# The start of a decoder layer: norm gain spread on chip, identity made on chip, loads issued in another order

## The chip, the cores and the metric

The kernel runs on 8 cores of one Trainium2 chip. Each core computes one of the eight sequences of the batch, and all eight run the same program. The metric is the device time in microseconds (us) of the slowest core. The time before is 937.29 us, the median of 3 runs (936.63 to 937.66).

## What is computed

One decoder layer over x of 2048 tokens by 1024, per sequence, cut to what matters here:

```python
h = rms_norm(x, norm_mix)                  # x * rsqrt(mean(x^2) + eps) * norm_mix
q, k, v, u, g_a, g_p = split(h @ w_in)     # q, k, v, u: 512 columns each
q = partial_rope(rms_norm(q_heads, q_norm)); k = partial_rope(rms_norm(k_heads, k_norm))
o_attn = block_sparse_attention(q, k, v)   # 8 heads of 64, blocks of 256, top 3 blocks
o_pool = multiscale_pool(u)
x = x + (sigmoid(g_a)*(o_attn@w_up_attn) + sigmoid(g_p)*(o_pool@w_up_pool)) @ w_out
x = x + relu(rms_norm(x, norm_mlp) @ w_ff1)^2 @ w_ff2
```

The change touches only the first stage: the norm of x, its transposition, and the projections to q, k, v and u.

## The kernel before, in words

**Helpers.** A class `Trk` keeps a semaphore for each engine and rings of semaphores for the DMAs of SyncE (`"sp"`) and of GpSimd (`"pool"`). Every operation goes through `t.op`, `t.group` (several matmuls that count as one) or `t.dma`; waits come from the buffers that an operation reads and writes. Each engine works through its own instructions in order. `t.wait_written(e, buf)` makes engine `e` wait until `buf` is written; everything behind it on that engine waits too.

**The work of the first stage.** x comes as 16 tiles of 128 tokens (512 KB of float32 each) into four slots (`p0_load`, SyncE's queue). For each tile ScalarE squares and sums it and takes the root (`p0_sq`, L388 and L391), VectorE takes the reciprocal (L397) and multiplies the tile by it and by the gain `gmix_bc` (`p0_mul`, L399). The bf16 result is transposed, for the first nine tiles by eight TensorE transposes (`p0_tr`, L406) that need the identity `ident_b` and a copy out of PSUM (`p0_ev`, L377 or L372), for the others by a DMA transpose. Then each of the four column groups K, V, Q and U has one job per tile: eight matmuls of 512 columns (`proj_mm`, L433), the first four with the first half of the weights, the other four with the second half. So there are 64 jobs. K and Q jobs are followed by a norm per head, a rotation and a transpose (L439 to L487), K and V and U by evictions.

**The weights** come by casting DMAs on GpSimd's queue, float32 in memory and bf16 on chip, two halves for each of K, V, Q and U (`load_w`; 512 KB written by each half).

**The order.** `first_loads` issues by hand what comes first. On SyncE: x tile 0, the gain `gmix_bc` (the 1024 gains copied to 128 rows by the host, 512 KB), then a wait for the first half of K's weights, then x tiles 1 and 2, three small tables (`c_small`, `c_gv`, `c_rope`) and x tile 3. On GpSimd: the identity (from memory), K's weights, five memsets (`pool_setup`, L353 and L355), a wait for x tile 1, V's weights.

All else is ordered by a planner that runs while the program is built. It gives each task a cost, an engine and an earliest time (`W_AT` for jobs by column group, `X_AT` for the first x tiles, `after` for others), simulates the five engines, and emits the tasks in the order of their simulated starts. Its numbers set only the order of the instructions; on the chip they wait for data. In its order, V's job of a tile lies 3 tiles behind K's, Q's 7 and U's 12. From tile 4 on a load of x waits for the multiplication that frees its slot. Q's weights are issued when the load into slot 0 that precedes them in program order (tile 4) has landed (`load_w_after`), U's with slot 1 (tile 5). When the projections near their end, the attention's steps begin (L907, L945).

Of the kernel before, what the change touches and what calls it, by code (L numbers as in the profile page):

```python
# [33 lines left out]
class Trk:  # L34
    def __init__(self, nc, es, n_ring=12):
# [9 lines left out]
        for q in ("sp", "pool"):  # L45
# [106 lines left out]
def build_nc():  # L152
    nc = bass.Bass("TRN2", target_bir_lowering=False)

    def din(name, shape):
# [21 lines left out]
    with es:  # L177
# [133 lines left out]
        b_wgTf, b_wgT, b_gmix_bc = Buf("wgTf"), Buf("wgT"), Buf("gmix_bc")  # L311
# [83 lines left out]
        def p0_mul(tt, s2):  # L395
# [6 lines left out]
                reads=[b_xslot[sl], b_rstd1[tt], b_gmix_bc], writes=[b_hb0[s2]])  # L402
# [221 lines left out]

        def first_loads():
            t.op("dve", lambda e: e.memset(eps_c, EPS), writes=[b_eps])
            t.op("dve", lambda e: e.memset(ones_b, 1.0), writes=[b_ones])
            p0_load(0)
            t.dma("pool", ident_b, c_ident_d, writes=[b_ident])
            t.dma("sp", gmix_bc, gmix_vec_d, writes=[b_gmix_bc])  # L630
            load_w(CG_K)
            pool_setup()
            t.wait_written("sp", b_wqkvu[CG_K][0])
# [6 lines left out]
            t.wait_written("pool", b_xslot[1])  # L640
# [8 lines left out]
        W_AT = {CG_K: 15.0, CG_V: 30.0, CG_Q: 43.0, CG_U: 54.0}  # L649
        X_AT = [4.7, 16.3, 18.6, 23.0]  # L650
# [822 lines left out]
```

How the kernel before makes its waits and increments, by code:

```python
    def _wait(self, e, need):  # L95
        eng = self.E[e]
        seen = self.seen[e]
        for k, v in need.items():
            if e == "pe" and k == "pe":
                continue
            if seen.get(k, 0) < v:
                eng.wait_ge(self.sems[k], v)
                seen[k] = v
# [9 lines left out]
    def op(self, e, fn, reads=(), writes=()):  # L113
        self._wait(e, self._need(reads, writes, e))
        ins = fn(self.E[e])
        self.cnt[e] += 1
        ins.then_inc(self.sems[e], 1)
        self._mark(e, self.cnt[e], reads, writes)
# [1 line left out]
    def group(self, e, fns, reads=(), writes=()):  # L120
        self._wait(e, self._need(reads, writes, e))
        ins = None
        for fn in fns:
            ins = fn(self.E[e])
        self.cnt[e] += 1
        ins.then_inc(self.sems[e], 1)
        self._mark(e, self.cnt[e], reads, writes)
# [1 line left out]
    def dma(self, q, out, in_, reads=(), writes=(), transpose=False):  # L129
        need = self._need(reads, writes)
        ring = self.rings[q]
        slot = ring["slots"][ring["i"] % len(ring["slots"])]
        ring["i"] += 1
        if slot[1] > 0:
            self._add(need, slot[0], slot[1])
        self._wait(q, need)
        if transpose:
            ins = self.E[q].dma_start_transpose(out=out, in_=in_)
        else:
            ins = self.E[q].dma_start(out=out, in_=in_)
        slot[1] += 16
        ins.then_inc(self.sems[slot[0]], 16)
        self._mark(slot[0], slot[1], reads, writes)
```

## Time and profile before

| what | value |
|---|---|
| median of 3 runs | 937.29 us |
| the profiled execution, its own time | 936.56 us |
| its span on the slowest core (core 4) | 935.5 us, so 1.06 us lie around it |
| spans of the eight cores | 930.1 to 935.5 us |
| TensorE (matmul) busy | 899.7 us, 96% of the span |
| VectorE, ScalarE busy | 462.3 us (49%), 364.8 us (39%) |
| GpSimd busy | 111.8 us (12%) |
| data moved by DMA | 78.13 MB, mean 84 GB/s |

In the rows, PE is TensorE, PEld its weight loads, DVE VectorE, ACT ScalarE, POOL GpSimd, SP SyncE; a q behind a name is that engine's queue of instructions. A time is in us from the start of the span unless marked ns. L12 is a line of the kernel. A matmul that waits behind others in the pipeline counts as busy, so a busy PE need not be one at its peak. A row of the chain of waits names what the end of a stretch hung on, step by step.

### The profile page before, as it was taken

Reading aid. Unit: us, or ns where it says so; the run is one execution under the profiler, and the core shown is the slowest. Engines: PE = TensorE matmul, PEld = TensorE weight load, DVE = VectorE, ACT = ScalarE, POOL = GpSimd, SP = SyncE. Lnnn points to the kernel's source line nnn. Section 1 sums busy time; section 2 is a strip of 40 time slices with the busy share of each in tenths; the row PEclk is TensorE's granted clock in tenths of the full one; section 3 lists DMA queues with packets and bytes.
Section 4 is the critical chain, followed back from the end, with each engine's and each line's share of the span. In section 5 each row is a group of like instructions: output and inputs, shape, how many; then the busy total and the mean of one; then the engine's idle time right before and its main releaser. Section 6 shows DMA issues by size and latency. Waiting matters only on the chain.

```text
span 935.5 us, 17328 instructions; the slowest of 8 cores (930.1 to 935.5 us)
## 1 busy us (share of the span) xinstructions
PE 899.7 (96%) x5724; PEld 461.8 (49%) x5724; DVE 462.3 (49%) x870; ACT 364.8 (39%) x722; POOL 111.8 (12%) x197
## 2 busy tenths in 40 slices
PE   2899998999999999999999999999999999999998
PEld 1444454667777654444444444444444444444444
DVE  2788877647332233345774444444443444444443
ACT  3777455788999952221006223131101222111120
POOL 4212212221000000100201111001110111000000
PEclk9999999999999999999999999999999999999999
DMA  7963353244533363993996433023330333202113
GB/s 186 226 160 80 64 136 46 53 63 75 70 69 66 61 102 98 203 197 83 159 142 99 56 48 55 12 32 48 56 46 1 46 47 56 34 1 82 54 68 157
DMA packets 66342, 78.13 MB, mean 84 GB/s; under 512 B 35984, under 2 KB 54672, under 8 KB 66000
## 3 DMA queue, kind: packets, MB, share of 16 engines
q0 software_dynamic: 25056, 40.28, 28.9%
q1 hardware_dynamic: 41200, 36.75, 16.5%
q8 instruction: 48, 0.79, 0.3%
q14 instruction: 38, 0.31, 0.1%
HBM read 98.41 MB, written 8.39 MB: 114 GB/s over the span
## 4 chain that ended last, share of the span: by engine, by line
PE 88%; DMA 6%; DVE 2%; issue 1%; ACT 1%; SPq 0%; POOL 0%; DVEq 0%; ACTq 0%; POOLq 0%
PE bank L1370 24%; PE bank L1341 24%; PE bank L1013 11%; PE bank L433 8%; PE bank L1241 6%; PE bank L907 6%; PE bank L945 3%; DMA raw<-w_qkvu 3%; PE bank L1027 3%; PE bank L1032 3%; DMA raw<-x 2%; DMA raw<-w_slice 1%; PE bank L487 1%; PE bank L520 0%; DVE raw L377 0%
## 5 line engine op out<-in xcount | busy, mean ns | idle before, releaser
L1370 PE MATMUL bank<-raw 128*128 128x512 bf16 (+1 forms) x1032 | 223.2, 377 | 0.0
L1341 PE MATMUL bank<-raw 128*128 128x512 bf16 x1024 | 223.1, 379 | 0.0
L1348 ACT ACTIVATE raw<-bank 128x512 f32<-128x512 f32 x128 | 76.4, 597 | 375.6 <-PE bank L1341 317.0
L1370 PEld LDWEIGHTS bank<-raw 128*128 128x128 bf16 x1032 | 101.1, 98 | 120.2
L1341 PEld LDWEIGHTS bank<-raw 128*128 128x128 bf16 x1024 | 100.1, 98 | 120.9
L1350 DVE SCALAR_TENSOR_TENSOR raw<-bank,raw 128x512 bf16<-128x512 f32 x128 | 88.5, 692 | 140.0 <-ACT raw L1348 140.0
L914 ACT ACTIVATE raw<-bank 128x512 bf16<-128x512 f32 (+1 forms) x288 | 145.0, 580 | 24.6 <-PE bank L945 20.6
L1378 DVE SCALAR_TENSOR_TENSOR raw<-bank,raw 128x512 f32<-128x512 f32 x129 | 96.3, 746 | 113.5 <-PE bank L1370 112.8
L433 PE MATMUL bank<-raw 128*128 128x512 bf16 x512 | 121.2, 386 | 10.9 <-ACT raw L372 3.8
L1013 PE MATMUL bank<-raw 128*128 128x512 bf16 x512 | 123.0, 380 | 2.1 <-DMA raw<-w_slice 1.9
L907 PE MATMUL bank<-raw 128*128 128x256 bf16 x576 | 98.7, 268 | 0.8 <-ACT raw L914 0.3
L140 POOL DMA_DIRECT2D raw<-w_ff x64 | 44.9, 702 | 347.2 <-PE bank L1341 184.9
L945 PEld LDWEIGHTS bank<-raw 128*128 128x128 bf16 x1088 | 69.9, 98 | 26.0 <-issue 1.0
L945 PE MATMUL bank<-raw 128*128 128x65 bf16 x1088 | 80.0, 194 | 0.8 <-DVE raw L954 0.7
L433 PEld LDWEIGHTS bank<-raw 128*128 128x128 bf16 x512 | 47.7, 98 | 66.0 <-issue 17.4
L1038 DVE SCALAR_TENSOR_TENSOR raw<-raw,bank 128x512 f32<-128x512 f32 x64 | 43.7, 685 | 71.5 <-PE bank L1032 53.8
L1013 PEld LDWEIGHTS bank<-raw 128*128 128x128 bf16 x512 | 49.4, 98 | 51.0 <-issue 3.2
L1018 ACT ACTIVATE raw<-bank 128x512 f32<-128x512 f32 x64 | 38.2, 597 | 75.2 <-PE bank L1013 73.9
L1241 PE MATMUL bank<-raw 128*128 128x512 bf16 x256 | 55.4, 379 | 0.0
L1241 PEld LDWEIGHTS bank<-raw 128*128 128x128 bf16 x256 | 25.0, 98 | 30.2
L907 PEld LDWEIGHTS bank<-raw 128*128 128x128 bf16 x576 | 37.1, 98 | 2.4 <-issue 1.2
L1027 PE MATMUL bank<-raw 128*128 128x512 bf16 x128 | 32.9, 379 | 0.0
(90 smaller groups left out, 578.2 us busy)
## 6 DMA issues: line engine op xcount, KB each, us to landing
raw<-x SPq DMA_DIRECT2D x32, 512.0 KB, 7.0
raw<-w_ff POOLq DMA_DIRECT2D x64, 256.0 KB, 4.0
raw<-w_slice POOLq DMA_DIRECT2D x22, 640.0 KB, 7.9
out<-raw SPq DMA_DIRECT2D x15, 512.0 KB, 2.7
raw<-w_qkvu POOLq DMA_DIRECT2D x8, 512.0 KB, 13.2
raw<-raw SPq DMA_DIRECT2D x2, 1024.0 KB, 4.5
raw<-w_out POOLq DMA_DIRECT2D x4, 512.0 KB, 13.1
raw<-c_ind POOLq DMA_DIRECT2D x4, 256.0 KB, 5.2
```

What stands on the lines that cost most here:

```text
L433: t.group("pe", [lambda e, c=c: e.matmul(bank_f(bk), lhsT=hT[:, c, tt * 128:(tt + 1) * 128], rhs=wqkvu[cg][:, c, :], start=(c == 0), stop= ...
L907: fns.append(lambda e, kt=kt, j=j, qa=qa: e.matmul(bank_f(sb_)[:, j * 256:j * 256 + 256 - qa], lhsT=ksel[:, pr, kt * 128:(kt + 1) * 128], ...
L914: t.op("act", lambda e: e.activation(out=pt[:, 0:nc_], in_=bank_f(sb_)[:, 0:nc_], func=AF.Exp, scale=0.125), reads=hb[sb_], writes=[b_PT[s ...
L945: fns.append(lambda e, dst=dst, c0_=c0_, kt=kt, ql=ql, last=last: e.matmul(dst, lhsT=pt[:, c0_:c0_ + 128], rhs=v_aug[:, kt, h, :], start=( ...
L1013: t.group("pe", [lambda e, c=c: e.matmul(bank_f(bk), lhsT=w[:, c, :], rhs=hT[:, c, T0:T0 + 512], start=(c == 0), stop=(c == 7)) for c in c ...
L1027: t.group("pe", [lambda e, c=c: e.matmul(bank_f(bk), lhsT=w[:, c, :], rhs=o_attnT[:, c, T0:T0 + 512], start=(c == 0), stop=(c == 3)) for c ...
L1241: t.group("pe", [lambda e, c=c, bk=bk, hf=hf: e.matmul(bank_f(bk), lhsT=mT[tt // 4][:, c, (tt % 4) * 128:(tt % 4 + 1) * 128], rhs=wout[:, ...
L1341: t.group("pe", [lambda e, c=c, j=j, bk=bk: e.matmul(bank_f(bk), lhsT=ffw1[s][:, c, j * 128:(j + 1) * 128], rhs=hT[:, c, tg * 512:(tg + 1) ...
L1348: t.op("act", lambda e, bk=bk, si_=si_: e.activation(out=sqz[si_], in_=bank_f(bk), func=AF.Square), reads=hb[bk], writes=[b_sqz[si_]])
L1350: t.op("dve", lambda e, bk=bk, si_=si_, j=j: e.scalar_tensor_tensor(out=a1T[ab][:, j, :], in0=bank_f(bk), scalar=0.0, in1=sqz[si_], op0=AL ...
L1370: t.group("pe", [lambda e, j=j, bk=bk, i=i, c0_=c0_, c1_=c1_, n_=n_: e.matmul(bank_f(bk)[:, 0:n_], lhsT=a1T[ab][:, j, i * 128:(i + 1) * 12 ...
L1378: t.op("dve", lambda e, bk=bk, dst=dst, tt=tt, n_=n_: e.scalar_tensor_tensor(out=dst, in0=bank_f(bk)[:, 0:n_], scalar=r2sq[:, tt:tt + 1], ...
```

## The change

1. The host passes the 1024 gains as [8, 128] (4 KB) in place of [128, 1024]. They are loaded into `g8` by a DMA on ScalarE's queue. VectorE splits them into three bf16 parts (three copies, two subtractions, each 8 x 128), TensorE spreads them over 128 rows with 24 matmuls (three for each 128 columns; the left operand is a column of the identity, read 128 times), and VectorE copies the two PSUM banks to `gmix_bc`.
2. The identity isn't loaded: GpSimd makes it with a memset and two affine selects, ahead of K's weights.
3. ScalarE runs a one-column Square of `eps_c` first of all, so that its table load doesn't wait for x.
4. On SyncE x tiles 1 and 2, the tables and x tile 3 no longer wait for K's weights. On GpSimd V's weights wait for the second half of K's and no longer for x tile 1. U's weights wait for slot 2 (tile 6) in place of slot 1.
5. The K jobs of tiles 0 and 1 are two tasks each, one for each half of the weights.
6. The planner's earliest times are lower: for K's jobs 12.5 in place of 15 (their first halves 9), for V, Q and U 6 lower each, for x tiles 1 to 3 8.2, 11.5 and 15.5 in place of 16.3, 18.6 and 23.0. VectorE counts as free from 7.

```diff
-        for q in ("sp", "pool"):
+        for q in ("sp", "pool", "act"):
...
-    gmix_vec_d = din("gmix_bc", [128, D])
+    gmix_vec_d = din("gmix", [8, 128])
-    c_ident_d = din("c_ident", [128, 128])
...
+        def spread_gain():
+            src, bsrc = g8, b_g8
+            for i in range(3):
+                t.op("dve", lambda e, i=i, src=src: e.tensor_copy(out=g8p[i], in_=src),
+                     reads=[bsrc], writes=[b_g8p[i]])
+                if i < 2:
+                    t.op("dve", lambda e, i=i, src=src: e.tensor_tensor(
+                        out=g8r[i], in0=src, in1=g8p[i], op=ALU.subtract),
+                        reads=[bsrc, b_g8p[i]], writes=[b_g8r[i]])
+                    src, bsrc = g8r[i], b_g8r[i]
+            for hf in range(2):
+                bk = gbank[hf]
+                fns = []
+                for c in range(4 * hf, 4 * hf + 4):
+                    for i in range(3):
+                        fns.append(lambda e, c=c, i=i, bk=bk: e.matmul(
+                            bank_f(bk)[:, (c % 4) * 128:(c % 4) * 128 + 128],
+                            lhsT=ident_b[0:8, c:c + 1].to_broadcast([8, 128]), rhs=g8p[i],
+                            start=(i == 0), stop=(i == 2)))
+                t.group("pe", fns, reads=[b_ident] + b_g8p, writes=hb[bk])
+                evict(("dve", "dve")[hf], gmix_bc[:, hf * 512:hf * 512 + 512], bank_f(bk), hb[bk], [b_gmix_bc[hf]])
+            for i in range(3):
+                b_qtok[i].fence = {"pe": t.cnt["pe"], "dve": t.cnt["dve"]}
         def first_loads():
             t.op("dve", lambda e: e.memset(eps_c, EPS), writes=[b_eps])
             t.op("dve", lambda e: e.memset(ones_b, 1.0), writes=[b_ones])
+            t.op("act", lambda e: e.activation(out=junk[:, 0:1], in_=eps_c, func=AF.Square),
+                 reads=[b_eps], writes=[b_junk])
+            t.dma("act", g8, gmix_vec_d, writes=[b_g8])
             p0_load(0)
-            t.dma("pool", ident_b, c_ident_d, writes=[b_ident])
-            t.dma("sp", gmix_bc, gmix_vec_d, writes=[b_gmix_bc])
+            t.op("pool", lambda e: e.memset(ident_b, 1.0), writes=[b_ident])
+            t.op("pool", lambda e: e.affine_select(
+                out=ident_b, in_=ident_b, pattern=[[1, 128]], compare_op=ALU.is_ge, fill=0.0, base=0,
+                channel_multiplier=-1), reads=[b_ident], writes=[b_ident])
+            t.op("pool", lambda e: e.affine_select(
+                out=ident_b, in_=ident_b, pattern=[[-1, 128]], compare_op=ALU.is_ge, fill=0.0, base=0,
+                channel_multiplier=1), reads=[b_ident], writes=[b_ident])
             load_w(CG_K)
+            spread_gain()
             pool_setup()
-            t.wait_written("sp", b_wqkvu[CG_K][0])
             p0_load(1)
             p0_load(2)
...
             p0_load(3)
-            t.wait_written("pool", b_xslot[1])
+            t.wait_written("pool", b_wqkvu[CG_K][1])
             load_w(CG_V)
...
-        W_AT = {CG_K: 15.0, CG_V: 30.0, CG_Q: 43.0, CG_U: 54.0}
-        X_AT = [4.7, 16.3, 18.6, 23.0]
+        K0_AT = 9.0
+        W_AT = {CG_K: 12.5, CG_V: 24.0, CG_Q: 37.0, CG_U: 48.0}
+        X_AT = [4.7, 8.2, 11.5, 15.5]
...
-            gains[is_k] = add("gains", pr_, [("dve", 0.85, lambda is_k=is_k: setup_gains(is_k))], after=20.5)
+            gains[is_k] = add("gains", pr_, [("dve", 0.85, lambda is_k=is_k: setup_gains(is_k))], after=14.5)
...
+            if cg == CG_K and tt < 2:
+                ph = Task("half", ji - 0.5, [], deps=[hev[tt]], get=["pj"], after=K0_AT)
+                ph.opts = [("pe", 0.87, lambda ji=ji, k_=ph: proj_mm(ji, k_.slots["pj"], (0,)))]
+                tasks.append(ph)
+                pj.deps, pj.get, pj.slots = [ph], [], ph.slots
+                pj.opts = [("pe", 0.87, lambda ji=ji, k_=pj: proj_mm(ji, k_.slots["pj"], (1,)))]
...
-        add("wq", 4.0, [("pool", 2.0, lambda: load_w_after(CG_Q, 0))], deps=[muls[1]], after=26.0)
-        add("wu", 8.0, [("pool", 2.0, lambda: load_w_after(CG_U, 1))], deps=[muls[2]], after=34.0)
+        add("wq", 4.0, [("pool", 2.0, lambda: load_w_after(CG_Q, 0))], deps=[muls[1]], after=25.0)
+        add("wu", 8.0, [("pool", 2.0, lambda: load_w_after(CG_U, 2))], deps=[muls[3]], after=34.0)
...
-        eng_free = {"pe": 0.0, "act": 0.0, "dve": 0.0, "pool": 20.0, "sp": 22.0}
+        eng_free = {"pe": 0.0, "act": 0.0, "dve": 7.0, "pool": 14.0, "sp": 15.0}
```

## Rows read from the trace of the kernel before

**Rows 1.** Projection matmuls (L433) by 5 us: stretch, length, busy, count, clock, DMA share, GB/s

```profile
10.00:15.00 5.00, 1.86 (x4) 1.00 0.96 193
...
35.00:40.00 5.00, 2.45 (x11) 1.00 1.03 222
...
100.00:105.00 5.00, 4.94 (x23) 1.00 0.55 107
```

**Rows 2.** The chain of waits, 0 to 40 us: start, length, what

```profile
2.24 9.53 DMA raw<-w_qkvu
11.85 4.63 DMA raw<-x
...
17.53 16.87 DMA raw<-w_qkvu
...
35.86 0.47 PE bank L406 x8
36.33 1.73 PE bank L433 x8
```

**Rows 3.** The timeline, 0 to 34 us: start, length, what, idle before it

```profile
1.07 0.40 SPq L140 DMA_DIRECT2D raw<-x  x1
...
1.53 0.41 SPq L140 DMA_DIRECT2D raw<-gmix_bc  x1
...
3.54 7.92 POOL L355 MEMSET raw<- 128x2048 f32 x4
5.11 1.28 ACT L388 ACT_TABLE_LOAD   x1 [5.11 <-DMA raw<-x]
...
8.44 1.28 DVE L399 SCALAR_TENSOR_TENSOR raw<-raw 128x1024 bf16<-128x1024 f32 x1 [0.17 <-DVE raw L397]
...
9.98 1.01 PE L406 MATMUL bank<-raw 128*128 128x128 bf16 x8 [9.98 <-DVE raw L399]
...
12.04 1.86 PE L433 MATMUL bank<-raw 128*128 128x512 bf16 x4 [1.05 <-DVE raw L377]
...
15.44 1.87 PE L433 MATMUL bank<-raw 128*128 128x512 bf16 x4 [1.53 <-DMA raw<-w_qkvu]
...
17.01 1.06 POOL L140 DMA_DIRECT2D raw<-w_qkvu  x2 [5.54 <-DMA raw<-x]
...
23.57 1.06 ACT L388 ACTIVATE raw<-raw 128x1024 bf16<-128x1024 f32 x1 [1.35 <-DMA raw<-x]
...
25.15 0.22 DVE L474 TENSOR_TENSOR raw<-raw 128x64 f32<-128x64 f32 x1
25.47 0.23 DVE L477 TENSOR_TENSOR raw<-raw 128x64 f32<-128x64 f32 x1
...
27.36 1.06 POOL L140 DMA_DIRECT2D raw<-w_qkvu  x2 [9.29 <-DMA raw<-x]
...
27.86 1.89 PE L433 MATMUL bank<-raw 128*128 128x512 bf16 x8 [0.75 <-ACT raw L372]
```

**Rows 4.** DMA queues' packets, MB, share, in the microsecond from 7, 17, 22 and 23

```profile
q0 software_dynamic: 47, 0.14, 118.2%
...
q1 hardware_dynamic: 120, 0.05, 17.2%
...
q1 hardware_dynamic: 101, 0.35, 92.2%
...
q0 software_dynamic: 18, 0.07, 47.6%
```

**Rows 5.** The weights' DMA queue from 25 to 30 us

```profile
q0 software_dynamic: 156, 0.57, 67.4%
```

**Rows 6.** GpSimd: an instruction by form, and those of L477, duration min/median/max

```profile
L359 POOL TENSOR_SCALAR_AFFINE_SELECT raw<-raw 128x128 bf16<-128x128 bf16 x1 | 0.3, 293 | 0.1
...
L477 POOL TENSOR_TENSOR raw<-raw x11: 317/319/1284, 32.5 to 124.4; 128x64 f32<-128x64 f32 x11
```

**Rows 7.** Busy time from 60 to 80 us: PE, PEld, DVE, ACT, POOL

```profile
60.00:80.00 20.00, 19.26 (x118) 9.42 (x117) 17.63 (x46) 14.16 (x30) 5.92 (x13) 1.00 0.50 107
```

**Rows 8.** TensorE's timeline where the attention begins

```profile
151.04 0.33 PE L907 MATMUL bank<-raw 128*128 128x256 bf16 x2
```

More of the change, by code:

```diff
@@ L266, in build_nc @@
         gmix_bc = view(E0 + 2 * KB, [128, D], F32)
+        g8 = view(E0 + 14 * KB, [8, 128], F32)
+        g8r = [view(E0 + 14 * KB + 512, [8, 128], F32), view(E0 + 15 * KB, [8, 128], F32)]
+        g8p = [view(E0 + 15 * KB + 512 + i * 256, [8, 128], BF16) for i in range(2)]
+        g8p.append(view(E0 + 16 * KB, [8, 128], BF16))
         hb0 = [view(o_, [128, D], BF16) for o_ in (E0 + 6 * KB, E0 + 8 * KB, G0 + 3584)]
@@ L310, in build_nc @@
         b_ones, b_band, b_qz, b_tri, b_eps = Buf("ones"), Buf("band"), Buf("qz"), Buf("tri"), Buf("eps")
-        b_wgTf, b_wgT, b_gmix_bc = Buf("wgTf"), Buf("wgT"), Buf("gmix_bc")
+        b_wgTf, b_wgT = Buf("wgTf"), Buf("wgT")
+        b_gmix_bc = [Buf("gmix_bc%d" % i) for i in range(2)]
         b_xslot = [Buf("xslot%d" % i) for i in range(NXS)]
@@ L401, in p0_mul @@
                 op0=ALU.mult, op1=ALU.mult),
-                reads=[b_xslot[sl], b_rstd1[tt], b_gmix_bc], writes=[b_hb0[s2]])
+                reads=[b_xslot[sl], b_rstd1[tt]] + b_gmix_bc, writes=[b_hb0[s2]])
         def p0_tr(tt, s2, bk):
@@ L429, in build_nc, with proj_mm @@
         NJ = len(jobs)
-        def proj_mm(ji, bk):
+        def proj_mm(ji, bk, hfs=(0, 1)):
             cg, tt = jobs[ji]
-            for hf in range(2):
+            for hf in hfs:
                 t.group("pe", [lambda e, c=c: e.matmul(
@@ L623, in build_nc @@
                  "st": [0, 1, 2, 3], "x16": [0, 1], "qtok": [0, 1, 2], "u": list(range(NU)), "mb": [3]}
+        b_g8, b_g8r, b_g8p = Buf("g8"), [Buf("g8r%d" % i) for i in range(2)], [Buf("g8p%d" % i) for i in range(3)]
+        def spread_gain():
[21 more added lines that the diff above has]
+                b_qtok[i].fence = {"pe": t.cnt["pe"], "dve": t.cnt["dve"]}
         def first_loads():
@@ L1409, in _host_consts @@
 def _host_consts():
-    ident = np.eye(128, dtype=np.float32)
     half = 8
@@ L1429, in _host_consts @@
         band[:, g * 3 + 2, :] = main0
-    return ident, rope, band
+    return rope, band
 _CACHE = {}
@@ L1437 @@
     x = f(x)
-    ident, rope, band = _host_consts()
+    rope, band = _host_consts()
     gq, gk = f(q_norm)[0], f(k_norm)[0]
@@ L1458 @@
         "c_small": small, "c_gv": gv, "gmlp_bc": np.ascontiguousarray(np.broadcast_to(f(norm_mlp)[0], (128, D))),
-        "gmix_bc": np.ascontiguousarray(np.broadcast_to(f(norm_mix)[0], (128, D))),
-        "c_ident": ident, "c_rope": rope, "c_band": band,
+        "gmix": f(norm_mix)[0].reshape(8, 128),
+        "c_rope": rope, "c_band": band,
         "c_ind": ind4,
```

## The prediction

> **What bounds the kernel now.** The page says TensorE is busy for 96% of the span, so time can only come from stretches in which it isn't fed. I looked for them first with the projection matmuls counted by 5 us [rows 1]. Eight of them, a job, take 1.73 us when nothing waits [rows 2], so 23 fit into 5 us; the count is 4 from 10 to 15 us, 11 from 35 to 40 and 23 from 100 to 105. By 40.4 us six jobs (10.4 us), six tile transposes (0.47 each [rows 2], 2.8) and about 0.9 us of small ones are done: 14.1 us of work, so some 26.3 us are lost. From there to 151 us, where the attention's steps begin [rows 8], lie 110.6 us; 55 jobs take 95.2 of them and the transposes and band matmuls beside them about 12.5, so about 3 more are lost, 29.3 in all. A gain in the start therefore isn't eaten up by TensorE later: it works without gaps and only begins earlier. That is the main reason why I expect the whole span to follow.
>
> What the lost 26 us hang on is in the chain of waits [rows 2]: K's weights to 11.8 us, then x tile 1 (issued only after them), then V's weights, issued behind that tile and landed at 34.4 us. Three DMAs make up 31 of the first 34.4 us; VectorE and ScalarE are not in that part of the chain. The timeline [rows 3] gives the steps between: the table load begins only when x tile 0 is there (5.11), first multiplication at 8.44, first projection matmul at 12.04, second half of K at 15.44.
>
> **How fast the two DMA queues are.** The queue of x alone moves about 100 packets of 4 KB per us (a tile is 128), the weights' queue alone 47 in the stretch shown, some of them small, and with both at work the weights get 156 in 5 us, 31 per us [rows 4, 5]. A column group's weights are 256 packets, so 8.3 us of data. K's ran from about 5.3 to 14.1 with x mostly absent, 8.8 us, which is no faster. So letting x in beside K costs K little. That is where I chose: the bound on the good side is K's second half at 15.0 us, on the bad side a K that waits behind x (a rival below).
>
> Two more facts of the same rows. At 17 us the x queue is at 17%: the small tables hold x tile 3 up while nothing else runs. And V, issued at 17.01 [rows 3], has its first 18 packets only in the stretch from 23 us [rows 4], 6 us later, when the x tiles queued ahead of it are nearly through. K's issue at 2.24 had its first at about 5.3, when x tile 0 and the gain (issued at 1.07 and 1.53) were through. I read both as: a weight load starts about 3 us after its issue, or when the x packets queued before it have drained, if that is later.
>
> The Trainium skill (DMA: Bandwidth & Descriptors, Queues, rings and completion order) says that each DMA engine goes round between its queues packet by packet. By that alone V would have started 3 us after its issue. From 25 us on the trace agrees (31 of each per us); for the start it doesn't. With the round alone, V's data would begin 1 us sooner than I take below, and the sum would be 1 us lower.
>
> **The parts.**
>
> *Gain spread.* Removed: 512 KB from x's queue (128 packets, 1.3 us at 100 per us). Added on the path of tile 0: ScalarE's table load from about 1.25 to 2.55 and a short Square, DMA issue to about 3.1. No such small transfer on a queue of its own is in the trace. x tile 0 was issued at 1.07 and there at 5.11, 4.0 us with 1.8 us of data, so 2.2 without them; the old gain took 5.5 us behind it. So it lands between 5.3 and 8.6; I take 5.3, as it has no data to speak of. Five dependent VectorE operations of 128 columns: between the 0.06 us of a one-column memset and the 0.32 us from one start to the next of L474 and L477 [rows 3]; I take 0.32, the nearest, 1.6 us, so 6.9. 24 matmuls of 128 columns at the slow pace of the first transposes (8 in 1.01, so 0.11 apart [rows 3]): 2.6 us, and the last copy out 0.69: about 10.4. Then reciprocal and the multiplication, which began at 8.44 before: 10.8 now. The transposes and copy that follow put the first projection matmul at 14.4 in place of 12.04. This part makes the start 2.4 us later. It costs nothing in the sum, because the second tile's multiplication could not begin before 18.5 then (tile 1 landed at 16.5 [rows 2]) and now tile 1 is there at about 7, where the gain landed before. Without that cover it would cost 2.4.
>
> *Table load.* 1.28 us [rows 3] leave the path of tile 0, but that path now ends in the gain. Worth 0.
>
> *Identity.* One DMA issue (0.68) goes; a memset (0.2) and two selects (0.29 each [rows 6]) plus their hand-overs come, ahead of K's issue: between 0.3 sooner and 0.5 us later. I take 0.1 later. GpSimd's memsets, 7.92 us, move with it and still end before V's issue.
>
> *x tiles at once.* SyncE's issues of tiles 1 and 2, the tables and tile 3 now run from about 1.5 us. Tile 1 takes the place of the gain (7), tile 2 comes at about 11, the tables by 16, tile 3 at 17.5 in place of 23.5, tile 4 (once the first multiplication has freed its slot, 12) at about 20 in place of 27.3 [rows 3].
>
> *V behind K.* K's data start at 5.4, take 8.3 us and land 1.4 us after their last packet (as 15.44 lay behind 14.1), so its second half lands at 15.2, the issue of V follows at 15.7 in place of 17.01. x tiles 3 and 4 are ahead of it and drain by 19.5; data to 27.8, landed at about 29.2 in place of 34.4. Q and U follow on the same queue without a gap, as they did. **This is the term that counts: 5.2 us.**
>
> *TensorE between 14.4 and 29.2.* K jobs of tiles 0 to 4: 8.65 us, five tile transposes 2.35, four head transposes 1.2, and the slow pace: the first 16 matmuls were 0.43 apart in place of 0.22 (4 in 1.86 at 12.04, 8 in 1.89 at 27.86 [rows 3]; 1.2 GHz and then 2.4 GHz, the column of the granted clock being at 1.00 in both), so up to 4.3 us. Together 16.5 us for 14.8 us: TensorE is just fed. Its lost time would then be 14.4 + 4.3 and 4.5 us of later gaps (the 3 of before and 1.5 for a late x tile), 23.2, against 29.3 before: 6.1 us. The two countings give 5.2 and 6.1; I take 5.2, the one that has its end in a DMA. Halves of K jobs: they let four matmuls run before K's second half; in my times the second half is there (15.2) before the first has run (16.2), so nothing.
>
> **Sum.** The profiled execution took 936.56 us (span 935.5): 936.56 - 5.2 = 931.4. The median of the runs is 0.73 higher than that execution, so I forecast 932.1.
>
> **Rivals.**
> - *V's wait only moves* (0.16). If V starts 6.3 us after its issue as before, whatever is ahead, it gains only the 1.3 us of its issue; TensorE is then ahead by a job or so of K (1.73): 3.0 us, 934.3. For it: only one such start is in the trace. Against: the K load started in 3 us.
> - *Port between VectorE and GpSimd* (0.10). Shown: L477 on GpSimd took 1284 ns once in place of 319, under a 1.28 us multiplication on VectorE [rows 6]. Under the four memsets (1.98 us apart) the three copies of the gain split could each wait for one to end: the chain ends near 9.5 in place of 6.9 and the first projection is at 17. Of the 2.6 us some 2 would be lost: 934.1. Against: the multiplication at 8.44 ran its normal 1.28 under a memset. The Trainium skill (SBUF — State Buffer, Who interferes with whom) has it as an exclusive lock for one-source copies between SBUF tiles; no row before has such a copy.
> - *VectorE is the true bound of the stage* (0.09): it is busy for 17.63 of the 20 us from 60 to 80 [rows 7]. Then an earlier TensorE only waits more: under 1 us gained, 936.6. Against: VectorE starts earlier as well.
> - *Slower: K behind x* (0.06). If K's packets wait until all x packets issued before them are through (tiles 0 to 3 and the rope table, 640 packets at 100, and the tables' stall of 2.7 us), they start at 11.8 in place of 5.3, K lands at 22, V is issued at 22.5 and lands near 38: 3.6 us later than now, 940.9. It decides from the point where K's second half lands later than about 17.5. The start rule above leans this way; against it, SyncE needs about 0.45 us for each issue and is not far ahead of GpSimd's issue.
> - The rest (0.59) is the forecast, with 0.06 of it beyond 7.8 us, should TensorE be fed from 12 us.
>
> **Range.** Low end 929.5 (7.8 us gained: the 6.1 of the second counting, 1 for the start of V's data and some luck in the new order); high end 936.0 (the two middle rivals with 1.5 us against them). About 0.06 lie below and 0.13 above. Within 0.2% (1.9 us, about what a measurement of this kernel can tell from no change) counts the VectorE rival and a rest of the first: 0.11; slower 0.06; faster 0.83.
>
> **What the profile after would show.** First multiplication near 10.8 and first projection near 14.4; tile 1's square at about 7; V landed at 29 in place of 34.4; over 30 projection matmuls before 30 us in place of 25 or so; no x queue at 17% alone; attention's first step 5 us earlier than 151. I am wrong if V lands after 32 us, if K's second half lands after 17.5, or if gaps between 40 and 150 us grow beyond 3 us.

## The result, and the profile after

The kernel after takes 945.83 us (median of 4 runs, 943.94 to 974.86); the kernel before, timed beside it, 937.34. The ratio is 1.0085, with an interval of 1.0065 to 1.0105. (At 974.86 the cores of one die ran at a lower clock; ratios leave such executions out, medians don't.) The change makes the kernel about 8 us **slower**; the forecast was 932.1.

| what | before | after |
|---|---|---|
| the profiled execution, its own time | 936.56 us | 945.19 us |
| span of the core shown | 935.5 (core 4) | 943.5 (core 6) |
| first projection matmul | 12.04 | 17.20 |
| K's weights landed, halves 1 and 2 | 11.8 and 15.3 | 14.2 and 20.1 |
| V's weights landed, halves 1 and 2 | 29.6 and 34.4 | 28.2 and 33.3 |
| first halves of Q's and U's weights landed | 38.9, 48.3 | 38.2, 47.6 |
| x tiles 1, 2, 3, 4, 5 landed | 16.5, 18.7, 23.5, 26.8, 31.5 | 7.1, 8.8, 21.6, 22.9, 24.1 |
| x tiles 8, 9, 12 landed | 45.7, 50.4, 59.0 | 43.2, 48.7, 58.2 |
| granted clock, mean of the core | 0.998 | 0.994 |

**The start.** The timeline of the kernel after, 0 to 34 us (start, length, what, the idle time before it and what ended that). It answers to [rows 3]. The lines have moved: L433 is now L437 (projections), L406 L410 (tile transposes), L388 L392 (square of x), L399 L403 (multiplication), L439 L443 (square of a K or Q job), L461 L465 (the last read of a job's PSUM bank), L907 L953.

```profile
1.27 1.28 ACT L659 ACT_TABLE_LOAD   x1 [1.27 <-DVE raw L658]
...
2.35 1.23 POOL L140 DMA_DIRECT2D raw<-w_qkvu  x2 [0.23 <-issue]
...
3.81 7.91 POOL L359 MEMSET raw<- 128x2048 f32 x4
...
5.06 0.97 DVE L635 CAST raw<-raw 8x128 bf16<-8x128 f32 x1 [3.83 <-DMA raw<-gmix]
...
6.52 1.43 DVE L635 CAST raw<-raw 8x128 bf16<-8x128 f32 x1
...
8.44 1.44 DVE L635 CAST raw<-raw 8x128 bf16<-8x128 f32 x1
...
10.02 2.71 PE L647 MATMUL bank<-raw 8*128 8x128 bf16 x24 [10.02 <-DVE raw L635]
...
13.70 1.28 DVE L403 SCALAR_TENSOR_TENSOR raw<-raw 128x1024 bf16<-128x1024 f32 x1
...
17.20 1.87 PE L437 MATMUL bank<-raw 128*128 128x512 bf16 x4 [1.05 <-DVE raw L401]
...
20.24 3.25 PE L437 MATMUL bank<-raw 128*128 128x512 bf16 x12 [0.32 <-DMA raw<-w_qkvu]
...
20.63 1.05 POOL L140 DMA_DIRECT2D raw<-w_qkvu  x2 [8.91 <-DMA raw<-w_qkvu]
...
33.45 0.81 PE L437 MATMUL bank<-raw 128*128 128x512 bf16 x3 [0.39 <-DMA raw<-w_qkvu]
```

The table load is off the path, as forecast. The three casts of 8 x 128 took 0.97, 1.43 and 1.44 us, each beside one of GpSimd's memsets: they end at 6.03, 7.95 and 9.87, each within 0.1 us of the end of a memset (5.95, 7.88, 9.80). So the first multiplication came at 13.70 (forecast 10.8). K's second half was there at 20.1 (forecast 15.2), so V's issue came at 20.63, 3.6 us *later* than before, and V landed at 33.3 (forecast 29.2). The core shown is a late one: over the eight cores K's second half landed between 16.8 and 20.3 (before: 15.1 to 16.0).

The DMA queues of the kernel after in the microsecond from 9 (packets, MB, share), in answer to [rows 4]:

```profile
q0 software_dynamic: 33, 0.14, 90.5%
q1 hardware_dynamic: 32, 0.00, 5.0%
```

K's queue (q0) had its first 5 packets in the microsecond from 7, when x tiles 0 to 2 were all but through, 5 us after the issue at 2.35; its steady stream begins at 7.9. From then on it got one packet for each of x's queue (q1), here the small tables, 32 packets that carry next to nothing. That alone didn't make K slow. In the three microseconds from 11 four cores (1, 3, 4, 7) moved 34 to 44 of K's 4 KB packets per us beside as many small ones, no fewer than K got alone before (27 to 44 per us from 8 to 12 us); on the other four, the shown one with them, K fell to 12 to 24. Why it did stays open.

**The stage.** Projection matmuls (L437) of the kernel after by 5 us, columns as in [rows 1]: length, busy, count, the same two for the weight loads, granted clock, DMA share, GB/s.

```profile
10.00:15.00 5.00, 0.00 (x0) 0.00 (x0) 1.00 0.94 97
...
35.00:40.00 5.00, 4.81 (x22) 1.84 (x20) 1.00 0.99 216
...
50.00:55.00 5.00, 3.45 (x17) 1.40 (x16) 1.00 1.01 233
55.00:60.00 5.00, 1.53 (x8) 0.49 (x5) 0.88 0.54 163
60.00:65.00 5.00, 3.57 (x8) 1.02 (x8) 0.50 0.42 129
65.00:70.00 5.00, 4.48 (x20) 1.91 (x21) 0.93 0.00 0
...
100.00:105.00 5.00, 4.26 (x20) 1.80 (x20) 1.00 0.27 52
```

From 35 to 40 us there are 22 matmuls where there were 11: the start is indeed ahead by then. But from 55 to 65 us there are 16, half of them at a granted clock of 0.50, TensorE's 1.2 GHz level. The kernel before has 45 there, at 1.00 (columns as in [rows 1]):

```profile
55.00:60.00 5.00, 4.55 (x22) 1.00 0.45 157
60.00:65.00 5.00, 4.84 (x23) 1.00 0.17 47
```

To see where the kernels part I count the start of the n-th projection matmul, the median of the cores whose trace has all 512:

```
n          1     33     65     97    129    193    257    449    512
before   12.3   33.2   44.1   51.8   60.1   76.1   93.3  141.1  158.4
after    17.2   32.0   40.8   49.4   64.7   80.6   99.7  146.5  166.6
later    +4.9   -1.2   -3.3   -2.4   +4.6   +4.5   +6.4   +5.4   +8.2
```

The 8.2 us at the end of the stage are about the loss of the whole kernel. **They are made of** a head start of 2.4 us at the 97th matmul, 7.0 lost up to the 129th, 1.9 from the 193rd to the 257th, 2.8 at the end (449th to 512th), and 1.1 won back between.

The first of these is the largest. TensorE's timeline and then ScalarE's, of the same stretch:

```profile
54.65 1.89 PE L437 MATMUL bank<-raw 128*128 128x512 bf16 x8
60.94 3.57 PE L437 MATMUL bank<-raw 128*128 128x512 bf16 x8 [4.41 <-DVE raw L465]
```

```profile
53.60 1.06 ACT L392 ACTIVATE raw<-raw 128x1024 bf16<-128x1024 f32 x1 [2.49 <-DMA raw<-x]
...
55.05 0.58 ACT L443 ACTIVATE raw<-bank 128x512 f32<-128x512 f32 x1
57.11 1.06 ACT L392 ACTIVATE raw<-raw 128x1024 bf16<-128x1024 f32 x1 [1.49 <-DMA raw<-x]
...
58.55 0.58 ACT L443 ACTIVATE raw<-bank 128x512 f32<-128x512 f32 x1
59.03 0.29 ACT L452 ACTIVATE raw<-raw 128x8 f32<-128x8 f32 x1
...
59.79 0.59 ACT L443 ACTIVATE raw<-bank 128x512 f32<-128x512 f32 x1
```

ScalarE waits for an x tile that has not landed (2.49 and 1.49 us) while the squares (L443) and roots (L452) of finished K and Q jobs stand behind it in its order. The job squared at 55.05 was summed by VectorE from 55.72 and got its root only at 59.03, behind the square of the x tile at 57.11. Without the root there is no scaling (L465), so the job's PSUM bank isn't freed, and TensorE stops for 4.41 us; its next eight matmuls take 3.57 us in place of 1.73. The chain of waits of the kernel after says it in one line (start, length, what), and has the second loss as well:

```profile
46.04 10.99 DMA raw<-x
57.11 1.16 ACT raw L392 x2
...
76.72 6.82 DMA raw<-x
```

**Why the order is wrong.** The order is the planner's, and the change lowered its numbers (part 6 of the change). Its own simulated times beside the chip's, for the square of an x tile, in us:

```
x tile                   3      9     10     11     12
before, planned       23.0   45.2   50.2   53.0   55.9
before, on the chip   23.6   50.5   54.8   57.8   60.1
after, planned        15.5   38.4   41.0   43.1   46.9
after, on the chip    22.4   48.8   53.6   57.1   60.3
```

Before, the plan was 4 to 5 us ahead of x; after, 10 to 14. On the chip tile 12 is squared at the same time in both.

### The profile page after: what moved, and what is told of

The parts are those of the page before. It is cut to its first block, busy times and chain, and to the rows that moved or that the text cites. A ratio compares the mean times of both kernels' runs of the same rounds, so it can differ in the third digit from the quotient of the medians.

```text
span 943.0 us, 17387 instructions; the slowest of 8 cores (939.2 to 943.5 us)
## 1 busy us (share of the span) xinstructions
PE 903.5 (96%) x5748; PEld 463.8 (49%) x5748; DVE 469.3 (50%) x884; ACT 366.7 (39%) x728; POOL 107.0 (11%) x187
## 4 chain that ended last, share of the span: by engine, by line
PE 88%; DMA 6%; DVE 3%; issue 2%; ACT 1%; POOL 0%; SPq 0%; DVEq 0%; ACTq 0%; POOLq 0%
PE bank L1416 23%; PE bank L1387 23%; PE bank L1059 11%; PE bank L437 8%; PE bank L953 6%; PE bank L1287 6%; PE bank L991 3%; DMA raw<-w_qkvu 3%; PE bank L1073 3%; PE bank L1078 3%; DMA raw<-x 2%; DMA raw<-w_slice 1%; PE bank L491 1%; PE bank L524 0%; DVE raw L381 0%
## 5 line engine op out<-in xcount | busy, mean ns | idle before, releaser
L437 PE MATMUL bank<-raw 128*128 128x512 bf16 x512 | 122.1, 389 | 14.4 <-DVE raw L465 7.9
L953 PE MATMUL bank<-raw 128*128 128x256 bf16 x576 | 98.6, 267 | 0.6 <-ACT raw L960 0.2
L437 PEld LDWEIGHTS bank<-raw 128*128 128x128 bf16 x512 | 47.9, 99 | 70.0 <-issue 22.2
L953 PEld LDWEIGHTS bank<-raw 128*128 128x128 bf16 x576 | 36.9, 97 | 2.0 <-issue 0.9
```

Of the source, the lines that this page charges most:

```text
L437: t.group("pe", [lambda e, c=c: e.matmul(bank_f(bk), lhsT=hT[:, c, tt * 128:(tt + 1) * 128], rhs=wqkvu[cg][:, c, :], start=(c == 0), stop= ...
L953: fns.append(lambda e, kt=kt, j=j, qa=qa: e.matmul(bank_f(sb_)[:, j * 256:j * 256 + 256 - qa], lhsT=ksel[:, pr, kt * 128:(kt + 1) * 128], ...
```

## The experiments

Sixteen runs, each a ratio to the kernel before timed in the same session; medians of different sessions are not compared with each other. In the later sessions the kernel before took 1.4 to 2.3 us more than in that of its profile (937.3), so differences under about 2 us from the row `before` in the tables below prove little.

**The change with the planner's old numbers** (`a_plan_old`), and the kernel before with the new ones (`b_plan_new`).

```diff
-        K0_AT = 9.0                                  # the kernel after
-        W_AT = {CG_K: 12.5, CG_V: 24.0, CG_Q: 37.0, CG_U: 48.0}
-        X_AT = [4.7, 8.2, 11.5, 15.5]
+        K0_AT = 12.0                                 # a_plan_old
+        W_AT = {CG_K: 15.0, CG_V: 30.0, CG_Q: 43.0, CG_U: 54.0}
+        X_AT = [4.7, 16.3, 18.6, 23.0]
```

Beside these, each took the other's `after` times, `eng_free` and slot for U's weights.

> The changed loads, spread gain and split K jobs, with the planner's numbers of the kernel before (first halves of K at 12). Theory 1, the order: the changed kernel is ahead of the one before up to the 97th projection matmul (49.4 against 51.8 us) and behind by 4.6 us at the 129th, after ScalarE sat in front of the squares of x tiles that had not landed; the new order assumes x and weights 6 to 7 us earlier than they come. With the old numbers the gap of 4.4 us near 56 us goes and the time falls to 934 to 938. Theory 2, the loads themselves (K's weights landing at 20 in place of 15.4, V's only 1 us sooner): the time stays at 943 to 946.

> The kernel before with only the planner's numbers of the changed one (and U's weights behind x slot 2); loads, gain and identity as before. Theory 1 (the order): slower than before by 5 to 9 us, 942 to 946, with a gap of some us near 55 us in front of a projection matmul. Theory 2 (the loads): within 2 us of before, 936 to 939.

Measured: a 943.61 us, ratio 1.0037 (1.0021 to 1.0052); b 948.43 us, 1.0096 (1.0074 to 1.0118). The numbers alone, on the old loads, cost as much as the whole change. In b, TensorE's timeline and ScalarE's have the same stop:

```profile
64.22 3.57 PE L433 MATMUL bank<-raw 128*128 128x512 bf16 x8 [4.20 <-DVE raw L461]
```

```profile
60.40 1.06 ACT L388 ACTIVATE raw<-raw 128x1024 bf16<-128x1024 f32 x1 [2.81 <-DMA raw<-x]
...
61.84 0.58 ACT L439 ACTIVATE raw<-bank 128x512 f32<-128x512 f32 x1
```

The old numbers don't fit the new loads either. In a, ScalarE squares tile 1, which landed near 7, only behind the square of the first K job, and that waits for K's late weights:

```profile
22.39 0.60 ACT L443 ACTIVATE raw<-bank 128x512 f32<-128x512 f32 x1 [16.09 <-PE bank L437]
22.89 1.05 ACT L392 ACTIVATE raw<-raw 128x1024 bf16<-128x1024 f32 x1
```

**The kernel before with half of the new numbers**: x's (`h_x_only`) or the weights' (`h_w_only`).

```diff
-        X_AT = [4.7, 16.3, 18.6, 23.0]               # h_x_only; "sp" also free from 15
+        X_AT = [4.7, 8.2, 11.5, 15.5]
-        W_AT = {CG_K: 15.0, CG_V: 30.0, CG_Q: 43.0, CG_U: 54.0}    # h_w_only
+        W_AT = {CG_K: 12.5, CG_V: 24.0, CG_Q: 37.0, CG_U: 48.0}
```

> The kernel before with only the planner's arrival times of x of the changed one (tiles at 8.2, 11.5, 15.5, SyncE free from 15). With all of the new numbers the kernel before took 9.6 us more. If it is the x times, this is slower by 6 to 10 us; if it is the weights' times, it is within 2 us of before. The planner puts the x squares at up to 13 us ahead of the landing with these, so I expect most of the loss here.

> The kernel before with only the planner's times of the weights of the changed one (12.5, 24, 37, 48). If the weights' times make the loss, slower by 6 to 10 us; else within 3 us: TensorE waits in its own queue for a job whose weights come 6 us later, but what stands behind it waits for tiles anyway.

Measured: 957.43 us, ratio 1.0184 (1.0154 to 1.0214), and 950.6 us, 1.0111 (1.0091 to 1.013). Numbers that only put the same instructions in another order cost up to 1.8%. x's half costs more than I expected and more than both halves together (b). Each has the same wait of ScalarE for x, first h_x_only, then h_w_only; TensorE's stops behind them are 5.66 and 2.78 us:

```profile
64.68 1.06 ACT L388 ACTIVATE raw<-raw 128x1024 bf16<-128x1024 f32 x1 [6.58 <-DMA raw<-x]
```

```profile
58.80 1.06 ACT L388 ACTIVATE raw<-raw 128x1024 bf16<-128x1024 f32 x1 [4.24 <-DMA raw<-x]
```

**All of the planner's numbers set to what the chip did** (`e_plan_true`), and **one of them alone** (`m_after_x43`), or that one and the first x tiles (`n_after_x_true`).

```diff
-        W_AT = {CG_K: 12.5, CG_V: 24.0, CG_Q: 37.0, CG_U: 48.0}    # e_plan_true
-        X_AT = [4.7, 8.2, 11.5, 15.5]
+        W_AT = {CG_K: 20.2, CG_V: 31.0, CG_Q: 40.0, CG_U: 50.0}
+        X_AT = [4.9, 7.2, 8.9, 21.7]                 # n_after_x_true too
...
-                x_ld[tt] = add("xld", pk - 9, [("sp", 2.6, lambda tt=tt: p0_load(tt))],
+                x_ld[tt] = add("xld", pk - 9, [("sp", 4.3, lambda tt=tt: p0_load(tt))],   # all three
```

> The changed kernel; only the planner's numbers are other ones, taken from where the changed kernel's data really land (x tiles 4.9, 7.2, 8.9, 21.7; K 15.5 and 20.2, V 31, Q 40, U 50; a later x load 4.3 us in place of 2.6; VectorE free from 13.4). Theory 1 (the order assumes data 6 to 13 us too early, so ScalarE waits for x tiles in front of work that TensorE needs): the 129th projection matmul comes at 58 to 61 in place of 64.7 us, the ratio to before falls from 1.0085 to 0.998 to 1.002. Theory 2 (what the loads do in the first 20 us costs by itself): the ratio stays above 1.004.

> The kernel after, with one number of the planner changed: a load of x from tile 4 on costs 4.3 us on its queue in place of 2.6. In the planner's own times the square of x tile 9 then stands at 43.6 (38.4 before this edit), tile 12's at 58.8 (46.9); on the chip the kernel after had them at 48.8 and 60.3. Theory (ScalarE's order runs ahead of x and TensorE stops for 4.4 us): the stop near 56.5 us goes, the 97th and 129th projection matmul are 10 to 12 us apart in place of 15.3, and the time is 939 to 942, a ratio of 0.999 to 1.003. Rival (it is the numbers of the weights and of the first four x tiles, which stay too early): the stop stays, 945. Second rival (the loads themselves cost the time): 945 too, but with the 97th to 129th matmul as in the kernel before.

> The kernel after, with the load cost of 4.3 us and the first x tiles planned where they land (4.9, 7.2, 8.9, 21.7), the weights' numbers left too early (K 9 and 12.5, V 24, Q 37, U 48). Theory: x's order is what counts, so this is within 0.15% of the run with all numbers true (939). Rival (the weights' early numbers alone cost, as in the old kernel with them, where they cost 1.1%): 943 to 948.

Measured: e 938.99 us, ratio 0.9992 (0.9978 to 1.0005); m 940.34 us, 1.0010 (0.9994 to 1.0025); n 941.48 us, 1.0023 (1.0011 to 1.0036). One number, the 2.6 us that the planner takes for a load of x, carries the most: with 4.3 the ratio falls from 1.0085 to 1.0010. ScalarE's and TensorE's timelines of m have neither the wait for x nor the stop:

```profile
52.43 1.05 ACT L392 ACTIVATE raw<-raw 128x1024 bf16<-128x1024 f32 x1
...
53.86 0.58 ACT L443 ACTIVATE raw<-bank 128x512 f32<-128x512 f32 x1
...
56.65 1.05 ACT L392 ACTIVATE raw<-raw 128x1024 bf16<-128x1024 f32 x1
```

```profile
54.17 5.34 PE L437 MATMUL bank<-raw 128*128 128x512 bf16 x24
```

The matmuls of these runs, n-th start as above:

```
n            1     33     65     97    129    193    257    449    512
before     12.3   33.2   44.1   51.8   60.1   76.1   93.3  141.1  158.4
after      17.2   32.0   40.8   49.4   64.7   80.6   99.7  146.5  166.6
a          17.2   38.9   48.1   56.2   64.2   84.0  102.2  149.0  166.3
b          21.2   35.1   43.4   52.0   66.7   82.6  102.2  149.0  168.5
e          17.6   33.0   41.4   50.0   60.0   77.4   93.9  141.9  159.2
m          17.2   32.3   43.4   51.9   59.9   78.3   95.6  142.9  163.3
n          17.4   36.2   44.4   52.8   60.9   76.8   94.3  141.8  162.6
```

The last column isn't the kernel's loss to the microsecond: a ends the stage 7.9 us later and the kernel is 3.5 us slower by its ratio, m 4.9 and 0.9; 1.4 to 1.6 us of that may be the sessions'. n was expected within 0.15% of e and isn't. The table shows where: at the 449th matmul n is level with e; the last 64 take 20.8 us in n, 20.4 in m and 20.1 in the kernel after, 17.3 in e and before.

**The hand-over to the attention** (`j_hand`, `k_g_hand`). That end loss is a second stop, in TensorE's timeline of the kernel after:

```profile
157.98 0.71 PE L953 MATMUL bank<-raw 128*128 128x256 bf16 x6
160.69 3.08 PE L437 MATMUL bank<-raw 128*128 128x512 bf16 x8 [2.01 <-DVE raw L465]
```

Six score matmuls stand together and the next job then waits 2.01 us for its bank, at a lower clock behind; before, the scores came two at a time, from 151.04 on [rows 8]. My theory was that the attention is begun too early in the plan.

```diff
-        T_ATT = last_root.end + LAT
+        T_ATT = last_root.end + LAT + 2.0            # k_g_hand: the same on g_loads
```

> The changed kernel with the attention's first steps put 2 us later into the order. In it the 449th projection matmul is 5.4 us later than before and the 512th 8.2, with a gap of 2.2 us near 158 us. If where the attention's steps are mixed in costs these 2.8 us, they go and the ratio falls by 0.002 to 0.003 from 1.0085; if the earlier loss is all, the ratio stays.

> The same 2 us in g_loads, where the 449th matmul was 1.0 us earlier than before and the 512th 1.7 later. If the hand-over costs it 2.7 us: ratio 0.997 to 0.999 in place of 1.0004. If not: 1.000 to 1.002.

Measured: 949.07 us, ratio 1.0108 (1.0079 to 1.0137), and 941.55 us, 1.0025 (1.0009 to 1.0041), no better than the kernels they started from. The theory falls: the last 64 matmuls still take 20.2 us in j.

What the slow ends have in common is a PSUM bank. The last five U jobs may use banks 6 and 7 alone (`pj.only = gbank`). Worked out from each kernel's own planner, the last Q job, whose bank is held until its scaling (L465), stands in one of these two or outside them, and the time of the last 64 matmuls goes by that without an exception:

```
last Q job in bank 6 or 7    after 20.1, b 19.5, c 20.4, d 21.0, g 20.0, h_x 20.1, j 20.2, k 21.3, m 20.4, n 20.8
last Q job in bank 4 or 5    before 17.3, a 17.3, e 17.3, h_w 17.6, i 17.4, l 17.3, o 17.3, p 17.3
```

The job that starts at 160.69 is the first of the five in bank 7, and it starts when the last Q job's L465 (159.87, 0.68 us) is through. So some 3 us of the kernel after, and most of what parts n from e, go with the bank that the rotation had reached, and not with how true the numbers are. No run changed the bank alone.

**The loads.** With the order set aside, is anything in the loads worth having? First the gain's casts on ScalarE (`c_act_cast`), and the tables behind x tile 3 (`d_tables_late`), both on the kernel after.

```diff
-                t.op("dve", lambda e, i=i, src=src: e.tensor_copy(out=g8p[i], in_=src),
+                t.op("act", lambda e, i=i, src=src: e.activation(out=g8p[i], in_=src, func=AF.Copy),
```

```diff
             p0_load(2)
+            p0_load(3)
             t.dma("sp", small_c, c_small_d, writes=[b_small, b_gcq, b_gck])
...
-            p0_load(3)
```

> The changed kernel with the three bf16 copies of the gain split on ScalarE in place of VectorE. If VectorE's copies wait for GpSimd's memsets (they took 0.97, 1.43 and 1.44 us for 128 columns of 8 rows), the copies take about 0.3 us each, the first gain matmul comes at 7.5 in place of 10.0 and the first projection at about 14.7 in place of 17.2; the second half of K still lands near 20, so the time changes by less than 1.5 us. If the copies are slow for another reason, they stay above 0.9 us.

> The changed kernel with the three small tables behind x tile 3 on SyncE. In the changed kernel the 256 small packets of two tables ran one by one with K's packets from 8 to 18 us and x tile 3 stood behind them (landed at 21.6). Here x tile 3 lands by about 11, K's first packet comes 1 to 1.5 us later (9), K lands at 21, the tables at 20 to 22. If the loads of the first 20 us are what costs (theory 2), 2 to 3 us are gained by the earlier tile 3 or lost by the later K; by theory 1 (the order further on) the time stays within 1.5 us of 945.

Measured: c 944.8 us, ratio 1.0056 (1.0036 to 1.0075); d 945.93 us, 1.0068 (1.0043 to 1.0093). Two lines of c's timeline:

```profile
5.79 0.31 ACT L635 ACTIVATE raw<-raw 8x128 bf16<-8x128 f32 x1 [3.01 <-DMA raw<-gmix]
...
14.99 1.44 PE L437 MATMUL bank<-raw 128*128 128x512 bf16 x3 [1.05 <-DVE raw L401]
```

A cast takes 0.31 us on ScalarE in place of 0.97 to 1.44, and the first projection comes 2.2 us earlier; but from the 33rd matmul to the 97th c is within 0.1 us of the kernel after. In d, x tile 3 landed at 16.7 in place of 21.6 and V's issue came at 19.06; at the 97th matmul it is 0.9 us behind the kernel after. Neither interval lies apart from that of the kernel after.

Then **loads in an order that gives K its old place** (`g_loads`: tables on ScalarE's queue, x tile 1 with K, tiles 2 and 3 behind K's first half, casts on ScalarE, numbers to match), and **V issued right behind K** (`i_v_behind`: g without V's wait). On the mended order, the casts alone (`o_e_act`: e with them on ScalarE).

```diff
+            t.dma("act", small_c, c_small_d, writes=[b_small, b_gcq, b_gck])      # g_loads, i_v_behind
+            t.dma("act", gv_qk, c_gv_d.partition_broadcast(128), writes=[b_gv])
+            t.dma("act", rope_t, c_rope_d.rearrange("p (t n) -> p t n", t=NT), writes=[b_rope])
...
+            p0_load(1)
...
+            t.wait_written("sp", b_wqkvu[CG_K][0])
...
-            t.wait_written("pool", b_wqkvu[CG_K][1])                              # i_v_behind alone
```

> The changed kernel with other loads and true planner numbers for them: x tile 1 beside K, x tiles 2 and 3 after K's first half, the small tables on ScalarE's queue, the gain's copies on ScalarE. Expected: K lands at 12 and 15.5 as before, x tile 3 at 17.5, V issued at 16 and landed at 28, first projection near 14.5. Theory 1 plus 2: both costs gone, the last projection matmul 4 to 6 us earlier than before and the ratio 0.993 to 0.996. If the ratio is 1.0 or more, the stage's end isn't set by its first 30 us at all.

> The loads of g_loads, but V's weights are issued right behind K's and GpSimd's memsets (no wait), so the weights' queue has no hole (in the kernel before it had none of its packets from 14 to 23 us). Planner numbers for it (K 13 and 16.5, V 25, Q 34.5, U 43, x tiles 6, 8.3, 18, 22, then 4.2 us each). If the stage is set by when V, Q and U land: V lands at 21 to 26 in place of 30 to 35, the 65th projection matmul comes at 38 to 41 in place of 44.1, the last one 3 to 5 us earlier than before, the ratio 0.994 to 0.998. If it is set by the x tiles (31 packets per us beside weights) and the hand-over to the attention: ratio 0.999 to 1.003.

> The kernel after with all of the planner's numbers set to the landings (the run at 939.0) and the three gain copies on ScalarE, where they took 0.31 us each in place of 1.0 to 1.4. The first projection then begins near 15 in place of 17.6. If the start is worth what it gains: 937 (2 us less, since the second half of K lands at 20 whatever comes before, perhaps 1). If the stage is paced by x and its order (my theory now): within 0.1% of that run, 938 to 940.

Measured: g 940.43 us, ratio 1.0004 (0.9991 to 1.0016); i 941.25 us, 1.0019 (1.0004 to 1.0034); o 937.22 us, 0.9987 (0.9964 to 1.0009). g didn't give K its old place on every core: on core 4 K's halves landed at 13.2 and 16.6 and V's at 29.7 and 35.0, no earlier than before (29.6 and 34.4); the median of the eight is 18.1 for K's second half. It is 1.0 us ahead at the 449th matmul and loses that in the slow end. i has V's halves at 23.8 and 28.2 on core 4, about 6 us earlier, and then x tiles 2 to 5 only at 26.3 to 32.2, so TensorE has nothing to project; its timeline in i:

```profile
29.67 1.01 PE L410 MATMUL bank<-raw 128*128 128x128 bf16 x8 [7.77 <-DVE raw L459]
```

In o the first projection comes 3.0 us earlier than in e (14.6), the 512th 1.3 us (157.9); the intervals of the two overlap, and neither is apart from the kernel before. Why so little of a head start carries is one line in the chain of waits of e:

```profile
43.71 9.97 DMA raw<-x
```

From 44 to 54 us the chain hangs on x. o has the same line, 9.50 us from 41.20; g, m, n and l have none between 35 and 100 us, so it is not the rule for every order. e is 2.7 us ahead of the kernel before at the 65th matmul, 1.8 at the 97th, 0.1 at the 129th.

**The kernel before, its order alone made truer** (`l_before_x43`, and once more, `p_before_x43_again`).

```diff
-                x_ld[tt] = add("xld", pk - 9, [("sp", 2.6, lambda tt=tt: p0_load(tt))],
+                x_ld[tt] = add("xld", pk - 9, [("sp", 4.3, lambda tt=tt: p0_load(tt))],
```

> The kernel before with only the planner's cost of a later x load at 4.3 us in place of 2.6, what 31 packets per us beside the weights make of a tile of 128 packets (and near what the trace shows between landings from 27 to 55 us). If the order's misfit to the data is what costs, this is 0 to 2 us faster than before (its own x squares stood up to 5 us ahead of the landings); if the planner's numbers only shuffle the order by luck, it may be some us slower.

> The kernel before with only the planner's cost of an x load raised from 2.6 to 4.3 us, run once more on another chip: a ratio of 0.997 to 0.999 if the 0.22% gain of the first run is real, 1.000 if it was chance.

Measured: 937.22 us, ratio 0.9978 (0.9966 to 0.9991), and 936.67 us, 0.9974 (0.9961 to 0.9986). One number, with no part of the change, beats the kernel before by a quarter per cent, and no version of the change is apart below that (e 0.9992 and o 0.9987 overlap with it). The profiled executions don't show where: the 512th projection matmul starts at 158.8 and 158.9 (before 158.4, profiled in a faster session). That stays open.

## Why the prediction was wrong

**The step that failed** is the one I called my main reason: "A gain in the start therefore isn't eaten up by TensorE later: it works without gaps and only begins earlier." It was read from a trace in which it was true. It held because the planner's order fitted the old landings to within about 5 us, and the change moved that order too. What the runs showed in its place: TensorE was 2.4 us ahead at the 97th projection matmul, 4.6 us behind at the 129th and 8.2 behind at the 512th. I priced the planner's numbers nowhere in the sum. Their cost: 0.96% on the old loads (b), and with all of them true the 0.85% of the whole change goes to nothing (e); some 3 us of that go with the bank of the last Q job. The mechanism is a wait that no step of mine priced: that of all that is queued behind ScalarE's square of an x tile. The Trainium skill (PSUM — Partial Sum Buffer, Engine vs sequencer instructions) says that ScalarE's, VectorE's and GpSimd's queues are strict FIFO; the timeline agrees, L443 and L452 starting only when L392 is through, with their input ready.

**The head start isn't worth much even so.** I read the chain of waits only to 40 us. Had I read on, the kernel before has the same line (start, length, what):

```profile
50.24 7.52 DMA raw<-x
```

The DMA share of the kernel before is 1.02 to 1.04 in each 5 us from 20 to 55 us, and in the kernel after 0.99 to 1.05: the DMA engines are full, and x tile 12 lands at 58.2 in place of 59.0 though tile 1 is 9.4 us earlier. By these shares only bytes moved before 20 us, or not moved at all, would bring it forward. The gain's 512 KB and the identity's 32 are all that went; the stretch in which the x queue idled is now full of packets, but from 10 to 15 us they carry 97 GB/s in place of 193.

Point by point, by the prediction's own steps:

- *V behind K*, 5.2 us, "the term that counts": 1.1 us were measured (34.4 to 33.3). K's second half landed at 20.1, not 15.2. "Letting x in beside K costs K little" was wrong in the start, K beginning behind x tiles 0 to 2 (7.9 us, not 5.4). In the rate it was right on four cores; on the other four K fell to 12 to 24 of its packets per us for a while.
- *Start rule for weight loads* (3 us after the issue, or when the x packets queued before have drained): its second half fits, K's first packet coming when 371 of the 384 x packets queued before it had begun and V's when 754 of 768 had, and I should have applied it to K, where it gives 8 and not 5.4. The 3 us don't: V had its first packet 1.8 us after its issue. The Trainium skill (DMA: Bandwidth & Descriptors, Queues, rings and completion order), with its turn by turn, agrees with the 33 and 32 packets from 9 us on, and not with the start.
- *Slower: K behind x* (0.06, 940.9): the mechanism was right in half, K at 20.1 past the deciding point of 17.5, V's issue 3.6 us later. It didn't decide: V landed earlier than before all the same (first half 7.6 us after its issue in place of 12.6, with fewer x tiles queued ahead of it), and with the order mended the same loads cost nothing (e).
- *Port between VectorE and GpSimd* (0.10): happened, to the number forecast for the end of the three casts (9.9 against "near 9.5") and the first projection (17.2 against 17). Its price of 2 us isn't borne out: c gives the 2.2 us of the start back and is level with the kernel after at the 33rd matmul. The Trainium skill (SBUF — State Buffer, Who interferes with whom) has an exclusive lock for such copies; the trace agrees, the casts ending within 0.1 us of the memsets' ends.
- *Gain spread*: 0.32 us for each of five operations; the subtractions took 0.28, the casts 0.97 to 1.44. The 24 matmuls took 2.71 (forecast 2.6).
- *Table load* 0, *identity* 0.1 us (K's issue 2.35 in place of 2.24), *x tile 1 at 7*: right. *Halves of K jobs worth nothing*: not shown, no run takes them out; the reason given didn't hold, since K's second half landed (20.1) after the first had run (17.20).
- *TensorE between 14.4 and 29.2*: the slow pace of 16 matmuls at 0.43 in place of 0.22 is 3.4 us, not 4.3; it stands in the second counting alone.
- *V's wait only moves*, *VectorE is the true bound*: the first isn't what happened; VectorE was busy for 16.18 us from 60 to 80 (before 17.63 [rows 7]), so it had less to do in the kernel after, not more.

All three things by which I said I would be wrong came about: V after 32, K after 17.5, gaps beyond 3 us between 40 and 150.

## What to carry to other kernels

Where a planner or a hand-written order fixes what each engine does, its numbers are part of the change: compare its planned times with the landings in the trace, tile by tile, since an in-order engine that meets a tile 10 us too early holds up finished work behind it. Read the chain of waits to the end of the stage before valuing a head start; if the same DMA is on it later and the DMA share is at 1, the head start can end there. Where jobs take turns on a few buffers, look also at which buffer the turn has reached when the stage hands over. A stop of TensorE can cost more than its length: behind the one of 4.41 us eight matmuls ran at half the clock and took 1.84 us more, behind one of 1.87 us in the kernel before (at 40.37) sixteen took 3.61 us, the full pace.

## What the runs showed of the hardware

- Packets of two queues alternated one for one, whatever they carried: 33 of K's and 32 of the small tables' in the microsecond from 9 us. The same alternation went with 34 to 44 of K's packets per us on four cores and with 12 to 24 on the other four, from 11 to 14 us. x tile 3, queued behind the tables, landed at 21.6.
- A load on GpSimd's queue had its first packet only when the x tiles issued before it were nearly through on the cores shown: 5.4 us after its issue for K here, 6.0 for V before [rows 4], 1.8 for V here, when 754 of the 768 x packets ahead of it had begun.
- Casts on VectorE of only 8 partitions and 128 columns took up to 1.44 us beside GpSimd's memsets of 1.80 us each and ended within 0.1 us of their ends; on core 3 the first began at 5.79 and took 0.25. A subtraction between them took 0.28, and the same cast on ScalarE 0.31.
- Behind stops of 4.41 us (after) and 4.20 (b), eight matmuls took 3.57 us in place of 1.73; the clock was granted 0.50 from 60 to 65 us in the kernel after and was back at 1.00 from 70.
